# Dilated attention values: natural token tiles through a DRAM scratch, and the second scores of a group moved behind a projection half

## The chip, the cores and the metric

The kernel runs on one core of a Trainium2 chip. The metric is the device time of one execution in microseconds. Five engines run beside each other and meet only at semaphores: TensorE (PE: matmuls, and PEld: the loads of their stationary operand), VectorE (DVE), ScalarE (ACT), GpSimd (POOL) and the sync engine (SP), which here only issues transfers.

## What is computed

Two transformer blocks on 1024 tokens of width 1024, all in float32. The change lies in the second block, in its dilated attention: 24 heads of 64 in three groups of 8, with dilations 1, 4 and 16. Cut to what matters:

```python
DIL_CONFIGS = ((128, 1), (512, 4), (2048, 16))        # window, dilation
q_dil, k_dil, v_dil = h @ w_in[...]                    # 1536 columns each, 512 a group
q, k = rope(q), rope(k)                                # v is not roped
for g, (window, dilation) in enumerate(DIL_CONFIGS):
    # each query sees keys at offsets m * dilation, |m| <= window / (2 * dilation) = 64
    s = q @ k.T * D ** -0.5 ; p = exp(s - max) ; o = p @ v / sum(p)
out = softmax-weighted sum of the three groups
```

## The kernel before

The weights come in panels of 512 columns, in chunks of 512 KB, two chunks in staging. GpSimd splits each into a high and a low part, and a product is made of three passes (high by high, high by low, low by high). The normed input stands transposed in `h2T_hi` and `h2T_lo` (128 channels by 8 by 1024 tokens).

The dilated phase is a fixed list of **units** (`D_UNITS`, L476): for each group g its keys, values and queries, 8 units each, but 9 for group 0's values, so 73 units. A unit is one PSUM bank of 128x512 made by 24 matmuls (8 channel tiles by 3 passes) in two halves of 12, one half a **slot**. All engines walk through the same slots. `d_proj` (L1172) makes the half. Keys and queries have the weights as the stationary operand and 512 tokens moving. Values have the tokens as the stationary operand (`h2T`) and the 512 weight columns moving, so the output has tokens in partitions; a tile takes the 128 tokens that attention needs together (`value_tiles`, L450): for group 0 tiles shifted by 64, nine of them, for group 1 every fourth token, for group 2 every eighth. Banks rotate by three (`d_bank`), so unit u waits until unit u-3 was read (`d_read`).

After a unit, ScalarE copies it out (L1746 to L1760). A value unit goes straight into its tile of `vd` (named `v_dil`). A key or query unit goes into `ts` (`rope_in`, one buffer); SP then issues four transfers of 64 KB that swap the halves of each head into `rot` (`rope_swapped`, one buffer; `swap_halves`, L599), and VectorE multiplies by the sine table and adds to the cosine product (`rope_cos` L2265, `rope_sin` L2276). The next copy into `ts` waits for the swap (`swapped`), and the next swap waits until `rot` was used (`roped`).

Attention is cut into 16 **steps** a group (two heads, two query tiles). Steps begin some slots behind their query unit (`STEP_LAG`, L498). `d_scores` (L1197) waits for the roped queries and for the masking of the step before (`d_masked`), because all steps score into the same two banks. VectorE masks and takes the maximum (`d_soft`, L2286), ScalarE exponentiates (`d_exp`, L1725), TensorE transposes one slot later (`d_transposes`) and multiplies by the values two slots later (`d_values`). In a slot TensorE does the step's scores, the projection half, the values of the step two slots ago and the transposes of the step one slot ago; for the first step of a group the scores stand behind the half instead (L1247).

SP's loop (L668) does for each slot: the swaps of the unit before, the stores of the step two slots before, and in the first four units of each panel one weight chunk. Its queue is strictly in order.

Of the kernel before, what the change touches and what calls it, by code (L numbers as in the profile page):

```python
# [29 lines left out]
P = 128  # L30
# [67 lines left out]
def hybrid_blocks_kernel(nc, x, w_in, pool_w, pool_scale, attn_sinks, w_out, norm_pre, norm_post,  # L98
# [24 lines left out]
        "probs_copied": (("swa_pT", 16), ("d_pT", 48)),  # L123
        "values_summed": (("swa_valued", 16), ("d_valued", 48)),
        "values_copied": (("swa_out", 16), ("d_out", 48)),
        "pool_in_out": (("pool_c", 80), ("pool_spill", 64)),
    }
    for t in range(TT):
        shared[f"rows_in{t}"] = ((f"x_in{t}", 16),)
    for b in range(2):  # L130
        shared[f"x_tile_in{b}"] = ((f"x_back{b}", 64), (f"x1_back{b}", 64))
        shared[f"tile_out{b}"] = ((f"x1_out{b}", 64), (f"d_store{b}", 768))
# [76 lines left out]
    v_d = nc.dram_tensor("v_mla_scr", [S, 2 * H1 * HD], F32, kind="Internal").ap()  # L209
    am_d = nc.dram_tensor("amla_scr", [512, S], F32, kind="Internal").ap()  # L210
    dd_d = nc.dram_tensor("dilout_scr", [512, S], F32, kind="Internal").ap()
    dil_d = [nc.dram_tensor(f"dil{g}_scr", [S, 512], F32, kind="Internal").ap() for g in range(3)]
    st_d = [nc.dram_tensor(f"dil_stat{g}_scr", [S, STAT], F32, kind="Internal").ap() for g in range(2)]

# [225 lines left out]
    def tile_start(g, t):  # L440

        return ((P * t, 1), (t // 2 + 4 * P * (t % 2), 4), (t, 8))[g]

    def spread(start, step):
        return lambda h, k: h[:, k, start:start + step * (P - 1) + 1:step]

    def group_toks(g, t):
        return spread(*tile_start(g, t))

    def value_tiles(g):  # L450

        if g:
            return [(t, group_toks(g, t)) for t in range(TT)]
        starts = [0] + [P * t - HD for t in range(1, TT)] + [S - P]
        return [(t, spread(s_, 1)) for t, s_ in enumerate(starts)]

    def window(g, t):

# [6 lines left out]
        if t in (0, TT - 1):  # L465
# [7 lines left out]
    DIL_AT = 40  # L473
    OM_AT = 1

    D_UNITS = [(g, kind, t) for g in range(3) for kind in "kvq"  # L476
               for t in range(len(value_tiles(g)) if kind == "v" else 2 * 4)]
    N_D = len(D_UNITS)

    def rope_units(u):  # L480

        return sum(kind != "v" for _, kind, _ in D_UNITS[:u])

    def d_step(g, i):
        return 4 * 4 * g + i
# [28 lines left out]

    def d_bank(u):

        return (u + 2) % 3

    def gate_bank(u):

# [44 lines left out]
    def _(sp):  # L565
# [33 lines left out]
        def swap_halves(u):  # L599

            r = rope_units(u)
            sp.wait_ge(*after("d_copied", r + 1))
            if r:
                sp.wait_ge(*after("roped", r))
            for b in range(4):
                sp.dma_start(rot[32 * b:32 * b + 32, :], ts[32 * (b ^ 1):32 * (b ^ 1) + 32, :]).then_inc(sem("swapped"), 16)

        def d_rows(g, t):
            start, step = tile_start(g, t)
            return dil_d[g][start:start + step * (P - 1) + 1:step, :]  # L610
# [57 lines left out]
        for slot in range(D_SLOTS):  # L668
            u = slot // 2
            if slot % 2 == 0 and u in panel_start:  # L670
                place, start = slot, panel_start[u]
            done = unit_before(slot)
            if done and done[3] != "v":
                swap_halves(done[0])
            if slot - 2 in step_at:
                g, i = step_at[slot - 2]
                d_store(g, i)
                if i == 15 and g < 2:
                    stats_store(g)
            if (slot - place) % 2 and (slot - place) // 2 < 4 and u < N_D:  # L680
                load_chunk(start + (slot - place) // 2)
# [116 lines left out]
    def _(pe):  # L798
# [373 lines left out]
        def d_proj(slot):  # L1172

            u, part = divmod(slot, 2)
            g, kind, t = D_UNITS[u]
            name = f"{kind}{g}"
            s = index[name] % 2
            bank = ps[:, d_bank(u), :]
            if part == 0:
                if t == 0:  # L1180
                    panel_ready(name)
                if u >= 3:
                    pe.wait_ge(*after("d_read", u - 2))
            j, n = divmod(t, 2)
            for k in range(KT // 2 * part, KT // 2 * (part + 1)):
                if kind == "v":
                    toks = value_tiles(g)[t][1]
                    pairs = [(toks(a, k), b[:, s, k, :]) for a, b in ((h2h, wh), (h2h, wl), (h2l, wh))]
                else:
                    pairs = [(b[:, s, k, P * j:P * j + P], a[:, k, COLS * n:COLS * n + COLS])  # L1190
                             for a, b in ((h2h, wh), (h2l, wh), (h2h, wl))]
                for i, (a, b) in enumerate(pairs):
                    m = pe.matmul(bank, a, b, start=(k == 0 and i == 0), stop=(k == KT - 1 and i == 2))  # L1193
            if part == 1:
                m.then_inc(sem("d_done"), 1)
# [31 lines left out]
        def d_values(g, i):  # L1227
            n = d_step(g, i)
            j, tiles = step_of(g, i)
            if i == 0:  # L1230
                pe.wait_ge(*after("d_read", D_UNITS.index((g, "q", 0))))
            pe.wait_ge(*after("d_pT", n + 1))
            if n >= 1:
                pe.wait_ge(*after("d_out", n))
            c = 0
            for b, t in enumerate(tiles):
                blocks = window(g, t)[3]
                for a in range(2):
                    h, o = 2 * j + a, HD * (2 * b + a)
                    for kb, (_, _, vt, r0, nr) in enumerate(blocks):  # L1240
                        m = pe.matmul(ps[:, 7, o:o + HD], pTd[r0:r0 + nr, c, :],  # L1241
                                      vd[r0:r0 + nr, vt, HD * h:HD * h + HD], start=(kb == 0), stop=(kb == len(blocks) - 1))
                        c += 1
            m.then_inc(sem("d_valued"), 1)

        for slot in range(D_SLOTS):
            first = slot in step_at and step_at[slot][1] == 0  # L1247
            if slot in step_at and not first:
                d_scores(*step_at[slot])
            if slot < 2 * N_D:  # L1250
# [142 lines left out]
    def _(act):  # L1393
# [352 lines left out]
        for slot in range(D_SLOTS):  # L1746
            done = unit_before(slot)
            if done:
                u, r, g, kind, t = done
                if kind == "v" and t == 0:  # L1750
                    act.wait_ge(*after("d_read", u))
                    if g:
                        act.wait_ge(*after("d_valued", d_step(g, 0)))
                act.wait_ge(*after("d_done", u + 1))
                if kind == "v":
                    act.activation(vd[:, t, :], ps[:, d_bank(u), :], ACT.Copy).then_inc(sem("d_read"), 1)
                else:
                    if r:
                        act.wait_ge(*after("swapped", 64 * r))
                    act.activation(ts[:], ps[:, d_bank(u), :], ACT.Copy,  # L1760
                                   scale=HD ** -0.5 if kind == "q" else 1.0).then_inc(sem("d_copied"), 1)
            if slot in step_at:
                d_exp(*step_at[slot])
            if slot == D_SLOTS - 2:
# [700 lines left out]
```

## Time and profile before

| | |
|---|---|
| Median of 3 runs | 1717.63 us (1717.46 to 1717.9) |
| Profiled execution | 1716.55 us, span 1714.8 us |
| TensorE busy | 1685.3 us, 98% of the span |
| VectorE, ScalarE, GpSimd busy | 794.8, 586.3, 507.9 us |
| Dilated phase on TensorE | about 558 to 1140 us of the span |
| Bytes moved | 178.20 MB, mean 104 GB/s |

A busy time of TensorE adds up overlapping records less their overlap, so a record's length isn't the distance to the next matmul. A time in the views counts from the start of the span. "Idle before" is how long the engine stood before an instruction, with the one that released it. PEclk 1.00 means that the granted clock is the full 2.4 GHz, which it is in nearly all of this trace.

### The profile page before, as it was taken

Reading aid. Unit: us, or ns where it says so; the run is one execution under the profiler, and the core shown is the slowest. Engines: PE = TensorE matmul, PEld = TensorE weight load, DVE = VectorE, ACT = ScalarE, POOL = GpSimd, SP = SyncE. Lnnn points to the kernel's source line nnn. Section 1 sums busy time; section 2 is a strip of 40 time slices with the busy share of each in tenths; the row PEclk is TensorE's granted clock in tenths of the full one; section 3 lists DMA queues with packets and bytes.
Section 4 is the critical chain, followed back from the end, with each engine's and each line's share of the span. In section 5 each row is a group of like instructions: output and inputs, shape, how many; then the busy total and the mean of one; then the engine's idle time right before and its main releaser. Section 6 shows DMA issues by size and latency. Waiting matters only on the chain.

```text
span 1714.8 us, 22451 instructions
## 1 busy us (share of the span) xinstructions
PE 1685.3 (98%) x8753; PEld 1412.5 (82%) x8753; DVE 794.8 (46%) x1214; ACT 586.3 (34%) x1337; POOL 507.9 (30%) x400
## 2 busy tenths in 40 slices
PE   7999999999999999999999999999999999999998
PEld 6778778889878787888978889788787999988886
DVE  4330366344352213554166541645521888855714
ACT  5101456334333102441135310442113777741211
POOL 6125033023333333021220223015313744534310
PEclk9999999999999999999999999999999999999999
DMA  5113022233267422113131232227465525226332
GB/s 204 50 64 108 13 62 70 87 118 93 74 217 268 117 62 59 50 50 85 56 84 38 72 82 60 69 54 266 139 227 162 143 61 139 53 68 212 108 114 98
DMA packets 99290, 178.20 MB, mean 104 GB/s; under 512 B 16200, under 2 KB 36080, under 8 KB 99056
## 3 DMA queue, kind: packets, MB, share of 16 engines
q1 hardware_dynamic: 63280, 95.31, 20.0%
q10 hardware_dynamic: 35904, 81.44, 13.6%
q8 instruction: 70, 1.15, 0.3%
q14 instruction: 36, 0.29, 0.1%
HBM read 115.49 MB, written 48.63 MB: 96 GB/s over the span
## 4 chain that ended last, share of the span: by engine, by line
PE 95%; DVE 2%; ACT 1%; DMA 1%; issue 0%; SPq 0%; POOL 0%; ACTq 0%; POOLq 0%; DVEq 0%
PE ps L1193 23%; PE ps L1107 15%; PE ps L813 14%; PE ps L1045 5%; PE ps L1360 5%; PE ps L1300 5%; PE ps L1241 4%; PE ps L947 4%; PE ps L1330 3%; PE ps L1313 3%; PE ps L868 3%; PE ps L1209 2%; PE ps L1222 2%; PE ps L999 2%; PE ps L972 1%; PE ps L846 1%
## 5 line engine op out<-in xcount | busy, mean ns | idle before, releaser
L700 POOL TENSOR_SCALAR w_hi<-w_stage 128x1024 fp32r<-128x1024 f32 (+3 forms) x140 | 126.6, 911 | 997.7 <-PE ps L1193 361.1
L707 POOL TENSOR_TENSOR w_lo<-w_stage,w_hi 128x1024 fp32r<-128x1024 f32 (+3 forms) x140 | 270.1, 1937 | 8.9
L1193 PE MATMUL ps<-h2T_hi,w_hi 128*128 128x512 f32 x384 | 156.5, 408 | 0.7 <-ACT gate_tiles L1608 0.7
L1107 PE MATMUL ps<-h2T_hi,w_hi 128*128 128x512 f32 x384 | 154.2, 402 | 0.3 <-issue 0.3
L1193 PE MATMUL ps<-h2T_hi,w_lo 128*128 128x512 f32 x384 | 152.0, 396 | 0.0
L1107 PE MATMUL ps<-h2T_hi,w_lo 128*128 128x512 f32 x384 | 151.6, 395 | 0.0
L1193 PE MATMUL ps<-h2T_lo,w_hi 128*128 128x512 f32 x384 | 151.2, 394 | 0.0
L1107 PE MATMUL ps<-h2T_lo,w_hi 128*128 128x512 f32 x384 | 151.1, 393 | 0.0
L1735 ACT ACTIVATE probs_dil<-probs_dil,dil_stats_out 128x256 f32<-128x256 f32 (+2 forms) x192 | 87.6, 457 | 135.4 <-DVE dil_stats_out L2301 135.4
L1300 PE MATMUL ps<-k_mla,q_mla 128*128 128x512 f32 x384 | 104.0, 406 | 0.0
L2393 DVE TENSOR_REDUCE small<-ps 128x1 f32<-128x1024 f32 x64 | 77.7, 1214 | 54.8 <-PE ps L1300 54.8
L2273 DVE SCALAR_TENSOR_TENSOR qT_dil<-ps,cos_table_T 128x512 f32<-128x512 f32 x24 | 23.2, 967 | 166.9 <-ACT rope_in L1760 166.9
L732 POOL TENSOR_SCALAR p_mla<-p_mla,small 128x1024 f32<-128x1024 f32 x64 | 71.7, 1120 | 88.1 <-DVE small L2386 87.9
L1193 PEld LDWEIGHTS ps<-h2T_hi,w_hi 128*128 128x128 f32 x384 | 72.0, 188 | 26.6 <-issue 9.2
L2380 DVE TENSOR_TENSOR pT_mla_lo<-ps,pT_mla_hi 128x512 fp32r<-128x512 f32 x128 | 81.9, 680 | 14.0 <-ACT pT_mla_hi L1848 14.0
L1848 ACT ACTIVATE pT_mla_hi<-ps 128x512 fp32r<-128x512 f32 x128 | 69.7, 596 | 52.2 <-PE ps L1313 52.0
L1107 PEld LDWEIGHTS ps<-h2T_hi,w_lo 128*128 128x128 f32 x384 | 72.1, 188 | 18.1
L1193 PEld LDWEIGHTS ps<-h2T_hi,w_lo 128*128 128x128 f32 x384 | 72.2, 188 | 17.6
L1107 PEld LDWEIGHTS ps<-h2T_hi,w_hi 128*128 128x128 f32 x384 | 72.1, 188 | 17.1 <-issue 0.4
L1241 PEld LDWEIGHTS ps<-v_dil,probsT_dil 128*128 128x128 f32 (+1 forms) x640 | 80.8, 191 | 6.4 <-ACT probsT_dil L1744 0.5
L1107 PEld LDWEIGHTS ps<-h2T_lo,w_hi 128*128 128x128 f32 x384 | 72.1, 188 | 16.4
L2280 DVE TENSOR_TENSOR rope_swapped<-rope_swapped,sin_table_T 128x512 f32<-128x512 f32 x48 | 43.8, 912 | 89.6 <-DMA rope_swapped<-rope_in 89.6
(296 smaller groups left out, 3814.1 us busy)
## 6 DMA issues: line engine op xcount, KB each, us to landing
w_stage<-in_w_in SPq DMA_DIRECT2D x76, 512.0 KB, 3.9
rope_swapped<-rope_in SPq DMA_DIRECT2D x192, 64.0 KB, 2.0
w_stage<-in_w_out SPq DMA_DIRECT2D x16, 512.0 KB, 3.8
gate_scr<-gate_tiles ACTq DMA_DIRECT2D x16, 512.0 KB, 3.5
gates<-gate_scr ACTq DMA_DIRECT2D x32, 256.0 KB, 3.6
dil_scr<-dil_out SPq DMA_DIRECT2D x96, 64.0 KB, 1.6
dil_nums<-dil_scr ACTq DMA_DIRECT2D x24, 256.0 KB, 4.0
x_back<-in_x ACTq DMA_DIRECT2D x8, 512.0 KB, 3.6
```

The costliest lines, as they stand in the source:

```text
L700: last = nc.gpsimd.tensor_scalar(hi_, raw_, 1.0, 0.0, ALU.mult, ALU.add)
L707: last = nc.gpsimd.tensor_tensor(lo_, raw_, hi_.bitcast(F32), ALU.subtract)
L813: m = pe.matmul(acc, a, b, start=(i == 0 and j == 0), stop=(i == len(pairs) - 1 and j == 2))
L1045: m = pe.matmul(ps[:, Y_BANKS[t % 4] + half, :], a[:, k, tk], b[:, s, k, :], start=(k == 0 and j == 0), stop=(k == KT - 1 and j == 2))
L1107: m = pe.matmul(ps[:, gate_bank(u), :], a[:, s, k, P * m_:P * m_ + P], b[:, k, COLS * n:COLS * n + COLS], start=(k == 0 and j == 0), stop= ...
L1193: m = pe.matmul(bank, a, b, start=(k == 0 and i == 0), stop=(k == KT - 1 and i == 2))
L1241: m = pe.matmul(ps[:, 7, o:o + HD], pTd[r0:r0 + nr, c, :], vd[r0:r0 + nr, vt, HD * h:HD * h + HD], start=(kb == 0), stop=(kb == len(blocks ...
L1300: m = pe.matmul(ps[:, 2 * (i % 2) + n, :], Q[:, a, q], K[:, b, COLS * n:COLS * n + COLS], start=(j == 0), stop=(j == 2))
L1360: m = pe.matmul(ps[:, u % 8, :], a, b, start=(k == 0 and j == 0), stop=(k == 3 and j == 2))
L1735: act.activation(p_, p_, ACT.Exp, bias=o[:, h:h + 1], accum_out=o[:, H1 + h:H1 + h + 1]).then_inc(sem("d_exp"), 1)
L2380: nc.vector.tensor_tensor(PTl[dst], ps[:, 4 + half, :].rearrange("p (j c) -> p j c", c=P), PTh[dst].bitcast(F32), ALU.subtract).then_inc(s ...
L2393: nc.vector.tensor_reduce(rstd[:, j % 8:j % 8 + 1], ps[:, 2 * (j % 2):2 * (j % 2) + 2, :].rearrange("p b c -> p (b c)"), AX_X, ALU.max, ne ...
```

## The change

Value tiles of all groups become the eight natural tiles of 128 consecutive tokens, so group 0 has one unit less and the phase 72 units; the stationary operand is no longer shifted or strided. ScalarE copies a value unit into `ts` (now shared with the queries and keys), after the store or swap of the unit before. SP stores the 256 KB to a DRAM scratch `vd_d` (`store_values`), and loads tiles of `vd` from there with the shift or stride in the row address (`load_values`, 25 loads in all; `tiles_loaded` says after which unit which tiles come). At the last value unit of group 0 these are 3 tiles, of group 1 five, of group 2 four, and four more follow the first query unit of group 2. These stand in SP's queue behind the store of that unit and ahead of the swaps of the next. `d_values` waits for the loads. The second step's scores of each group stand behind the projection half as the first's do.

```diff
+    vd_d = nc.dram_tensor("v_dil_scr", [S, 512], F32, kind="Internal").ap()
-    def value_tiles(g):
+    def value_rows(g):
         if g:
-            return [(t, group_toks(g, t)) for t in range(TT)]
-        starts = [0] + [P * t - HD for t in range(1, TT)] + [S - P]
-        return [(t, spread(s_, 1)) for t, s_ in enumerate(starts)]
+            return [tile_start(g, t) for t in range(TT)]
+        return [(0, 1)] + [(P * t - HD, 1) for t in range(1, TT)] + [(S - P, 1)]
-    D_UNITS = [(g, kind, t) for g in range(3) for kind in "kvq"
-               for t in range(len(value_tiles(g)) if kind == "v" else 2 * 4)]
+    D_UNITS = [(g, kind, t) for g in range(3) for kind in "kvq" for t in range(TT)]
+    def tiles_loaded(g, kind, t):
+        if kind == "v" and g == 0:
+            return [t - 1] if 0 < t < TT - 1 else [TT - 2, TT - 1, TT] if t else []
+        if kind == "v" and g == 1:
+            return [2 * (t - 4)] if 4 <= t < TT - 1 else [6, 1, 3, 5, 7] if t == TT - 1 else []
+        if g == 2 and (kind, t) in (("v", TT - 1), ("q", 0)):
+            return list(range(4, TT)) if kind == "q" else list(range(4))
+        return []
+        def store_values(u):
+            g, _, t = D_UNITS[u]
+            sp.wait_ge(*after("d_read", u + 1))
+            if g and t == 0:
+                sp.wait_ge(*after("v_moved", 16 * (9, 17)[g - 1]))
+            sp.dma_start(vd_d[P * t:P * t + P, :], ts[:]).then_inc(sem("v_stored"), 16)
+        def load_values(u):
+            g, kind, t = D_UNITS[u]
+            for tile in tiles_loaded(g, kind, t):
+                sp.wait_ge(*after("v_stored", 16 * (8 * g + (t if kind == "v" and t < TT - 1 else TT))))
+                if g:
+                    sp.wait_ge(*after("d_valued", d_step(g, 0)))
+                start, step = value_rows(g)[tile]
+                sp.dma_start(vd[:, tile, :], vd_d[start:start + step * (P - 1) + 1:step, :]).then_inc(sem("v_moved"), 16)
-            if done and done[3] != "v":
-                swap_halves(done[0])
+            if done:
+                (store_values if done[3] == "v" else swap_halves)(done[0])
+                load_values(done[0])
@@ d_proj
-                    toks = value_tiles(g)[t][1]
-                    pairs = [(toks(a, k), b[:, s, k, :]) for a, b in ((h2h, wh), (h2h, wl), (h2l, wh))]
+                    pairs = [(a[:, k, P * t:P * t + P], b[:, s, k, :]) for a, b in ((h2h, wh), (h2h, wl), (h2l, wh))]
@@ d_values
             if i == 0:
-                pe.wait_ge(*after("d_read", D_UNITS.index((g, "q", 0))))
+                pe.wait_ge(*after("v_moved", 16 * (9 + 8 * g)))
@@ TensorE's slots
-            first = slot in step_at and step_at[slot][1] == 0
+            first = slot in step_at and step_at[slot][1] < 2
@@ ScalarE's slots
-                if kind == "v":
-                    act.activation(vd[:, t, :], ps[:, d_bank(u), :], ACT.Copy).then_inc(sem("d_read"), 1)
-                else:
-                    if r:
-                        act.wait_ge(*after("swapped", 64 * r))
-                    act.activation(ts[:], ps[:, d_bank(u), :], ACT.Copy,
-                                   scale=HD ** -0.5 if kind == "q" else 1.0).then_inc(sem("d_copied"), 1)
+                if u and D_UNITS[u - 1][1] == "v":
+                    act.wait_ge(*after("v_stored", 16 * values_stored(u)))
+                elif u:
+                    act.wait_ge(*after("swapped", 64 * r))
+                act.activation(ts[:], ps[:, d_bank(u), :], ACT.Copy,
+                               scale=HD ** -0.5 if kind == "q" else 1.0).then_inc(sem("d_read" if kind == "v" else "d_copied"), 1)
```

## Rows read from the trace of the kernel before

**Rows 1.** The page: busy us, share of the span, instructions.

```profile
PE 1685.3 (98%) x8753; PEld 1412.5 (82%) x8753; DVE 794.8 (46%) x1214; ACT 586.3 (34%) x1337; POOL 507.9 (30%) x400
```

**Rows 2.** Weight loads of value units, groups 0 to 2: ns min/median/max, starts.

```profile
L1193 PEld LDWEIGHTS ps<-w_hi,h2T_hi x72: 187/188/192, 603.3 to 653.1; 128*128 128x128 f32 x72
...
L1193 PEld LDWEIGHTS ps<-w_lo,h2T_hi x64: 308/309/309, 810.4 to 854.9; 128*128 128x128 f32 x64
...
L1193 PEld LDWEIGHTS ps<-w_lo,h2T_hi x64: 324/329/336, 1008.7 to 1054.8; 128*128 128x128 f32 x64
```

**Rows 3.** Timeline of ScalarE, value copies: start, us, operation, idle before.

```profile
614.92 0.60 ACT L1756 ACTIVATE v_dil<-ps 128x512 f32<-128x512 f32 x1 [4.96 <-PE ps L1193]
...
654.28 0.60 ACT L1756 ACTIVATE v_dil<-ps 128x512 f32<-128x512 f32 x1 [5.02 <-PE ps L1193]
...
827.52 0.60 ACT L1756 ACTIVATE v_dil<-ps 128x512 f32<-128x512 f32 x1 [5.06 <-PE ps L1193]
...
855.78 0.60 ACT L1756 ACTIVATE v_dil<-ps 128x512 f32<-128x512 f32 x1 [5.05 <-PE ps L1193]
...
1026.39 0.60 ACT L1756 ACTIVATE v_dil<-ps 128x512 f32<-128x512 f32 x1 [5.24 <-PE ps L1193]
...
1055.78 0.60 ACT L1756 ACTIVATE v_dil<-ps 128x512 f32<-128x512 f32 x1 [5.29 <-PE ps L1193]
```

**Rows 4.** Timeline of TensorE: first, second, third scores of groups 0, 1, 2.

```profile
668.17 1.03 PE L1209 MATMUL ps<-kT_dil,qT_dil 64*128 64x192 f32 x8
...
670.46 1.13 PE L1209 MATMUL ps<-kT_dil,qT_dil 64*128 64x256 f32 x8 [1.26 <-DVE probs_dil L2294]
...
869.68 1.13 PE L1209 MATMUL ps<-kT_dil,qT_dil 64*128 64x256 f32 x8
872.21 1.13 PE L1209 MATMUL ps<-kT_dil,qT_dil 64*128 64x256 f32 x8 [1.39 <-DVE probs_dil L2294]
...
877.13 1.14 PE L1209 MATMUL ps<-kT_dil,qT_dil 64*128 64x256 f32 x8
...
1075.28 0.71 PE L1209 MATMUL ps<-kT_dil,qT_dil 64*128 64x128 f32 x8
...
1080.92 0.71 PE L1209 MATMUL ps<-kT_dil,qT_dil 64*128 64x128 f32 x8
```

**Rows 5.** Timelines of ScalarE (last exponential of step 0), then VectorE (rope).

```profile
673.40 0.19 ACT L1735 ACTIVATION_READ_ACCUMULATOR probs_dil<-probs_dil,dil_stats_out 128x1 f32 x1
...
867.24 1.09 DVE L2284 TENSOR_TENSOR qT_dil<-qT_dil,rope_swapped 128x512 f32<-128x512 f32 x1
...
1073.07 1.20 DVE L2284 TENSOR_TENSOR qT_dil<-qT_dil,rope_swapped 128x512 f32<-128x512 f32 x1
...
1078.19 0.69 DVE L2280 TENSOR_TENSOR rope_swapped<-rope_swapped,sin_table_T 128x512 f32<-128x512 f32 x1 [0.62 <-DMA rope_swapped<-rope_in]
```

**Rows 6.** Transfers by line: queue, count, KB each, median us from issue to landing.

```profile
rope_swapped<-rope_in SPq DMA_DIRECT2D x192, 64.0 KB, 2.0
...
dil_nums<-dil_scr ACTq DMA_DIRECT2D x24, 256.0 KB, 4.0
...
q_mla<-q_rope_scr SPq DMA_DIRECT2D x48, 64.0 KB, 3.9
...
zm_scr<-gate_tiles ACTq DMA_DIRECT2D x4, 512.0 KB, 2.7
```

**Rows 7.** Timeline of SP: swaps of group 1's first two query units.

```profile
862.01 2.41 SPq L606 DMA_DIRECT2D rope_swapped<-rope_in  x4
...
868.40 3.04 SPq L606 DMA_DIRECT2D rope_swapped<-rope_in  x4
```

**Rows 8.** Windows: us, busy of the five engines, PEclk, DMA share, GB/s.

```profile
860.00:862.00 2.00, 2.00 (x10) 1.61 (x9) 0.00 (x0) 0.60 (x1) 1.92 (x2) 1.00 0.73 190
...
1156.00:1158.00 2.00, 2.00 (x14) 1.68 (x12) 0.00 (x0) 0.55 (x3) 0.00 (x0) 1.00 0.94 330
```

More of the change, by code:

```diff
@@ L125, in hybrid_blocks_kernel @@
         "values_copied": (("swa_out", 16), ("d_out", 48)),
-        "pool_in_out": (("pool_c", 80), ("pool_spill", 64)),
+        "pool_in_out": (("pool_c", 80), ("pool_spill", 64), ("v_moved", 400)),
     }
@@ L129, in hybrid_blocks_kernel @@
         shared[f"rows_in{t}"] = ((f"x_in{t}", 16),)
+    shared["rows_in7"] += (("v_stored", 16 * 3 * TT),)
     for b in range(2):
@@ L442, in tile_start @@
         return ((P * t, 1), (t // 2 + 4 * P * (t % 2), 4), (t, 8))[g]
[L444 to L448, printed above, removed]
-    def value_tiles(g):
+    def value_rows(g):
         if g:
-            return [(t, group_toks(g, t)) for t in range(TT)]
-        starts = [0] + [P * t - HD for t in range(1, TT)] + [S - P]
-        return [(t, spread(s_, 1)) for t, s_ in enumerate(starts)]
+            return [tile_start(g, t) for t in range(TT)]
+        return [(0, 1)] + [(P * t - HD, 1) for t in range(1, TT)] + [(S - P, 1)]
     def window(g, t):
@@ L482, in rope_units, with values_stored @@
         return sum(kind != "v" for _, kind, _ in D_UNITS[:u])
+    def values_stored(u):
+        return sum(kind == "v" for _, kind, _ in D_UNITS[:u])
+    def tiles_loaded(g, kind, t):
[6 more added lines that the diff above has]
+        return []
     def d_step(g, i):
@@ L515, in d_bank @@
     def d_bank(u):
-        return (u + 2) % 3
+        return (u - N_D) % 3
     def gate_bank(u):
@@ L1751, in _ @@
                     act.wait_ge(*after("d_read", u))
-                    if g:
-                        act.wait_ge(*after("d_valued", d_step(g, 0)))
                 act.wait_ge(*after("d_done", u + 1))
-                if kind == "v":
-                    act.activation(vd[:, t, :], ps[:, d_bank(u), :], ACT.Copy).then_inc(sem("d_read"), 1)
-                else:
-                    if r:
-                        act.wait_ge(*after("swapped", 64 * r))
-                    act.activation(ts[:], ps[:, d_bank(u), :], ACT.Copy,
-                                   scale=HD ** -0.5 if kind == "q" else 1.0).then_inc(sem("d_copied"), 1)
+                if u and D_UNITS[u - 1][1] == "v":
[4 more added lines that the diff above has]
+                               scale=HD ** -0.5 if kind == "q" else 1.0).then_inc(sem("d_read" if kind == "v" else "d_copied"), 1)
             if slot in step_at:
```

## The prediction

> **What bounds the kernel now.** I read the busy times first: TensorE (PE) is busy for 1685.3 of 1714.8 us [rows 1]. So a change pays only by what it takes from TensorE's queue or from a gap in it. Transfers, ScalarE, VectorE and the sync queue count only where they make TensorE wait. The record of one 128x512 matmul lasts about 0.4 us, but matmuls overlap, so I don't price by that mean. I price a projection unit (24 matmuls) by the distance between two ScalarE copies in the value stretches, where each copy waits for TensorE alone [rows 3].
>
> **The removed ninth tile.** Group 0's values fall from nine units to eight. From the copy at 614.92 to the one at 654.28 are 7 units: 39.36 / 7 = 5.62 us each [rows 3]. TensorE runs through without a gap there, so the whole unit counts: **-5.62 us**.
>
> **Plain instead of strided weights.** In groups 1 and 2 the stationary operand of a value unit is every fourth or eighth token of `h2T`. Its load takes 309 ns at a step of 4 and 329 ns at a step of 8, against 188 ns plain [rows 2]. Most of that hides behind the moving 512 columns, as the copies show: group 1 has (855.78 - 827.52) / 5 = 5.65 us a unit, group 2 (1055.78 - 1026.39) / 5 = 5.88 us [rows 3]. With plain tiles both should come to group 0's 5.62: 8 x 0.03 = 0.24 us and 8 x 0.26 = 2.08 us, together **-2.3 us**. Bounds: 0 if the slower pace isn't from the stride, -2.5 us if the units come down to 5.60.
>
> The Trainium skill, SBUF — State Buffer, section on the DMA port swizzle, says that reads are at full speed while a 16-byte line is hit more than once and that fp32 can be strided by up to 4 for free. The load at step 4 disagrees (309 ns), though the unit it belongs to is nearly free. By that rule group 1 would give nothing and group 2 all, which is 0.24 us from my sum.
>
> **The detour through DRAM, value stretches.** Copies stay as long as they are (0.60 us, PSUM to SBUF), but go to the single buffer `ts`, so the copy of a unit now waits until the previous tile has been stored. The trace has no 256 KB store from SBUF; the nearest are 512 KB at 2.7 us and 64 KB swaps at 2.0 us [rows 6]. I take 2.2, near the swaps, with ends 2.0 and 2.7. The cycle copy 0.6, store 2.2 and two hand-overs of 0.1 (my estimate) is 3.0 us against 5.62 a unit: hidden, cost **0**, bounds 0 and 0, since the upper end also gives 3.5. The sync queue now waits for each unit in this stretch; behind it stand weight chunks, of which only four belong to eight units of 5.62 us, and a panel is first used one stretch later. The 24 stores and 25 loads of 256 KB are 12.8 MB of extra traffic beside 178 MB. Group 0's loads follow tile by tile and hide likewise.
>
> **The detour, at the turn to the queries.** Call C the end of the last value copy: 855.78 + 0.60 = 856.38 in group 1 [rows 3]. The sync queue now issues that tile's store at C+0.1, waits until it has landed (C+2.3), issues 5 loads in group 1 (3 in group 0, 4 in group 2), then one weight chunk of 512 KB, then the four swaps of the first query unit. A swap issue takes 2.41 / 4 = 0.6 us [rows 7]; at that pace 5 loads end at C+5.3 and the chunk at C+5.9, while the swaps issue at C+5.6 today. So the queue itself costs 0.3 us. The data matter more: strided 2 KB rows moved at 330 GB/s with engines 94% busy, so 351 GB/s full, and weight chunks with swaps at 190 / 0.73 = 260 GB/s [rows 8]. If the loads start to flow 1.5 us after issue, five take to C+3.8+3.7 = C+7.5 and the chunk to C+9.5; at 260 GB/s for the loads too it is C+8.8 and C+10.8. The swaps, which land at C+9.4 today (last issue 863.8 plus 2.0), would land by C+10.2 to C+11.5: late by 0.8 to 2.1 us. A 64 KB load in a crowd of others took 3.9 us instead of 2.0 [rows 6], which supports such a delay.
>
> What that costs: roped queries were ready at 867.24 + 1.09 = 868.33 [rows 5], the first scores began at 869.68 [rows 4], a cushion of 1.35 us. So the first scores start 0 to 0.75 us late. But the next swap waits for these roped queries (issued at 868.40 [rows 7]), VectorE's second masking waits for that swap, and TensorE's third scores wait for the masking. I estimate it as finished 7.65 us after the roped queries (4.5 to the landing of swaps that issue for 3.0 us [rows 7], 1.8 for sine and sum, 1.3 for the mask), so at 876.8 to 878.1 against 877.13 today [rows 4]. Group 1: bounds -0.6 (no delay at all, below) and +1.0; I take **-0.1**.
>
> Group 2 scores only after two query units. Its second unit is roped at 1073.07 + 1.20 = 1074.27 [rows 5], the scores begin at 1075.28 [rows 4], a cushion of 1.0 us. First unit: 4 loads, no delay in the queue, landing late by 0 to 1. After its swaps come 4 more loads and a chunk, 1.5 MB in all, then the second swap at C+12. At 351 GB/s they are gone before that swap's data come, at 260 GB/s they end near C+16.5 and delay it by about 1 us. The scores there already hang on this chain (sine at 1078.19 waits for a swap [rows 5]), so a delay costs in full: bounds 0 and +2.0, I take **+0.3**. In group 0, with 3 loads, the queue is free at C+4.7 and the data by C+8.5: **0**. The first value product waits for its tiles at no cost. It comes at least two slots (5.6 us) behind the first scores: in group 1 those stand at 869.68 = C+13.3, so from C+18.9 on, in group 2 (C = 1056.38) at 1075.28 = C+18.9, so from C+24.5 on [rows 3, 4]. The last load is issued by C+5.3 and C+10.4; 256 KB loads of such strided rows land in 4.0 us [rows 6], and even in a crowd by C+9 and C+17.
>
> **Second scores behind a projection half.** Today the second scores of a group wait for the masking of the first: TensorE stands idle 1.26 us in group 0 and 1.39 in group 1 [rows 4]. The half of 12 matmuls (2.8 us) now lies between, and the idle time is gone. But the transposes of the first step then come 1.1 + 2.8 + 1.1 = 5.0 us after the first scores began, and their exponentials are finished at 673.40 + 0.19 = 673.59, 5.4 us after 668.17 [rows 4, 5]: about 0.5 us comes back as a wait. Group 0 keeps **-0.75**. In group 1 it would keep -0.6, which stands in its line above. In group 2 the third scores (1080.92) hang on VectorE, which adds the third unit's sine before the second masking: 1078.19 + 0.69 + 1.2 + 0.75 = 1080.8 [rows 4, 5]. Whatever TensorE gains, it waits there: **0**.
>
> **Sum.** -5.62 - 2.3 - 0.75 - 0.1 + 0.3 = **-8.5 us**. The profiled execution took 1716.55 us (span 1714.8 and 1.75 around it), so it would take 1708.1; the median of the runs is 1717.63, 1.1 above it, which gives **1709.1 us**, and that is my prediction.
>
> **Rivals.**
> 1. *The swaps queue behind the loads.* If the sync queue's transfers are handled strictly in order and the new loads run slowly, group 1 and group 2 lose up to 2 us each more than I take and group 0 its 0.75: -8.5 + 5 = -3.5, so about 1714; the middle of the case is 1712. For it: 3.9 against 2.0 us [rows 6]. Against: the four query copies are a unit apart and 1.35 us of cushion stand ahead of the first scores. Chance 0.22. The Trainium skill, DMA: Bandwidth & Descriptors, section on queues, rings and completion order, says that one issuing engine has one ring on each of 16 DMA engines and that descriptors are taken in ring order. No row here shows that order directly; by it this rival gets the upper delays above, 1712.
> 2. *The transfers pass freely.* No swap is late: -5.62 - 2.3 - 0.75 - 0.6 - 0 = -9.3, with 5.60 a unit -9.6: 1708. Chance 0.20, and it lies inside my range.
> 3. *The stride isn't the cause of the slow units* (or plain value tiles are slower for another reason): -8.5 + 2.3 = -6.2: 1711.4. Against it is the jump of the load from 188 to 329 ns just there [rows 2]. Chance 0.05.
> 4. *Slower than before: the single buffer paces the value units.* If store and hand-overs take over 5.0 us, the cycle is longer than a unit; beyond 4.8 us of landing each unit pays the excess 24 times. At 5.6 us it is 24 x 0.8 = 19 us, so -8.5 + 19 = +10.5: 1728. It decides from 4.8 us, against 2.0 to 2.7 in the rows [rows 6]. The Trainium skill, same page, section on the anatomy of one DMA, gives 2.0 us plus bytes at 436 GB/s for another issue path; as an estimate 2.6 us for 256 KB, which leaves it hidden too. Chance 0.04.
>
> **Numbers.** Forecast (-7.5 to -9.2) 0.49, rival 1 0.22, rival 2 0.20, rival 3 0.05, rival 4 0.04. 0.2% (3.4 us) is about what a measurement of this kernel can tell from no change. Faster beyond that: forecast, rivals 2 and 3 and most of rival 1: 0.90; within: the poor end of rival 1: 0.05; slower: rival 4 and a rest for a wait that I haven't seen: 0.05. Range: 1706.5 (rival 2 and 1 us more) to 1714 (the end of rival 1).
>
> **What the profile after would show.** Value units 5.62 us apart in all three groups and all plain loads at 188 ns confirm the first two terms. The landing time of the value stores (I say 2.2 us) decides rival 4. The start of the first scores after the last value copy is 13.3 us in group 1 today; more means rival 1. A wait of some 0.5 us ahead of the first transposes in groups 0 and 1 shows the traded wait. I am wrong if TensorE shows waits inside the value stretches, or if the gap between the last value copy and the third scores grows by over 1 us in group 1 or 2.

## The result and the profile after

The changed kernel takes **1720.46 us** (median of 15 runs, 1716.67 to 1724.16) against 1717.15 us (15 runs, 1715.45 to 1719.23): ratio 1.0023, 95% interval 1.0016 to 1.0030. It is slower by 3.3 us; I had forecast 8.5 us less. The profiled execution took 1719.46 us with a span of 1717.6.

The two gains that I had priced are there. First TensorE's busy time as in [rows 1], then the weight loads of value units in groups 1 and 2 as in [rows 2], then value copies of groups 0 to 2 as in [rows 3] (last one of a group each, with ScalarE's idle time before it).

```profile
PE 1681.3 (98%) x8729; PEld 1389.7 (81%) x8729; DVE 798.6 (46%) x1214; ACT 585.9 (34%) x1336; POOL 509.8 (30%) x400
```

```profile
L1219 PEld LDWEIGHTS ps<-w_lo,h2T_hi x64: 187/188/192, 807.3 to 851.6; 128*128 128x128 f32 x64
...
L1219 PEld LDWEIGHTS ps<-w_lo,h2T_hi x64: 187/188/192, 1008.7 to 1052.9; 128*128 128x128 f32 x64
```

```profile
650.38 0.60 ACT L1783 ACTIVATE rope_in<-ps 128x512 f32<-128x512 f32 x1 [5.03 <-PE ps L1219]
...
852.51 0.60 ACT L1783 ACTIVATE rope_in<-ps 128x512 f32<-128x512 f32 x1 [5.03 <-PE ps L1219]
858.11 0.60 ACT L1783 ACTIVATE rope_in<-ps 128x512 f32<-128x512 f32 x1 [5.00 <-PE ps L1219]
865.66 0.60 ACT L1783 ACTIVATE rope_in<-ps 128x512 f32<-128x512 f32 x1 [6.95 <-DMA rope_swapped<-rope_in]
...
1053.84 0.60 ACT L1783 ACTIVATE rope_in<-ps 128x512 f32<-128x512 f32 x1 [5.03 <-PE ps L1219]
```

All loads are at 188 ns. The last value copies stand at 650.38, 852.51 and 1053.84 against 654.28, 855.78 and 1055.78 [rows 3]: earlier by 3.90, 3.27 and 1.94 us, although this execution started the dilated phase 1.73 us late (first copy at 566.21 instead of 564.48; more on this below). Counted from the phase's start that is 5.63, 5.00 and 3.67 us. So the kernel gains in the key and value stretches and loses in the query stretches. From a group's last value copy to the next group's first copy it takes 105.76 us instead of 104.86 in group 0 and 105.97 instead of 102.68 in group 1, and from group 2's last value copy to the last scores 95.08 instead of 89.56: 0.90, 3.29 and 5.52 us more. The third copy shown (858.11) is the first query unit's, and the next one (865.66) waits for a transfer, which none of these did in group 1 before.

Now the waits at the first scores, as in [rows 4]: TensorE's first scores of groups 0, 1 and 2, with the idle time before each and what ended it; then a matmul right behind the last.

```profile
665.24 1.03 PE L1235 MATMUL ps<-kT_dil,qT_dil 64*128 64x192 f32 x8 [0.90 <-DVE qT_dil L2307]
...
869.51 1.14 PE L1235 MATMUL ps<-kT_dil,qT_dil 64*128 64x256 f32 x8 [3.04 <-DVE qT_dil L2307]
...
1075.56 0.71 PE L1235 MATMUL ps<-kT_dil,qT_dil 64*128 64x128 f32 x8 [2.15 <-DVE qT_dil L2307]
...
1077.02 0.63 PE L1219 MATMUL ps<-h2T_hi,w_lo 128*128 128x512 f32 x1
```

Three waits for roped queries that didn't exist before. What delays them in group 1 is seen in three timelines: the sync queue (store of the last value tile, five loads, a weight chunk, the four swaps), VectorE (sine, then sum, of the first query unit) and GpSimd (the split of that chunk).

```profile
853.13 0.32 SPq L622 DMA_DIRECT2D v_dil_scr<-rope_in  x1
855.14 2.22 SPq L632 DMA_DIRECT2D v_dil<-v_dil_scr  x5
857.41 0.42 SPq L675 DMA_DIRECT2D w_stage<-in_w_in  x1
858.73 2.44 SPq L614 DMA_DIRECT2D rope_swapped<-rope_in  x4
```

```profile
865.60 0.74 DVE L2303 TENSOR_TENSOR rope_swapped<-rope_swapped,sin_table_T 128x512 f32<-128x512 f32 x1 [5.69 <-DMA rope_swapped<-rope_in]
866.38 3.08 DVE L2307 TENSOR_TENSOR qT_dil<-qT_dil,rope_swapped 128x512 f32<-128x512 f32 x1
```

```profile
864.75 1.05 POOL L727 TENSOR_SCALAR w_hi<-w_stage 128x1024 fp32r<-128x1024 f32 x1 [5.15 <-DMA w_stage<-in_w_in]
865.89 2.65 POOL L734 TENSOR_TENSOR w_lo<-w_stage,w_hi 128x1024 fp32r<-128x1024 f32 x1
```

With C = 852.51 + 0.60 = 853.11 as the end of the last value copy, the swaps are issued from C+5.6 on, as before, but have landed only at C+12.5 (865.60), not at C+9.5. Then the sum takes 3.08 us instead of 1.09 [rows 5]: it ends only after GpSimd's subtraction (865.89 to 868.54) is over. In the kernel before (C = 856.38), VectorE's sine, which starts when the swap has landed, stands at C+9.5; the split of that chunk began at C+6.7 instead of C+11.6 and its subtraction was over (866.66) when the sum began (867.24 [rows 5]):

```profile
865.89 1.31 DVE L2280 TENSOR_TENSOR rope_swapped<-rope_swapped,sin_table_T 128x512 f32<-128x512 f32 x1 [2.69 <-DMA rope_swapped<-rope_in]
...
863.12 1.04 POOL L700 TENSOR_SCALAR w_hi<-w_stage 128x1024 fp32r<-128x1024 f32 x1 [0.23 <-DMA w_stage<-in_w_in]
864.25 2.41 POOL L707 TENSOR_TENSOR w_lo<-w_stage,w_hi 128x1024 fp32r<-128x1024 f32 x1
```

The swap's 3.0 us and the sum's 2.0, less the cushion of 1.35 and 0.6 that the sine was shorter, give the wait of 3.04.

Group 2 loses more, and there the delay runs over two units. VectorE's sum of the first query unit, then the swaps of the second (C = 1053.84 + 0.60 = 1054.44; 1056.38 before):

```profile
1066.39 3.27 DVE L2307 TENSOR_TENSOR qT_dil<-qT_dil,rope_swapped 128x512 f32<-128x512 f32 x1
```

```profile
1069.73 2.41 SPq L614 DMA_DIRECT2D rope_swapped<-rope_in  x4
```

The first unit's swap has landed at C+11.2 instead of C+9.5, and its sum takes 3.27 us instead of 1.19, again beside GpSimd's subtraction (1065.89 to 1068.62). The second unit's swaps may only be issued after that sum, so they come at C+15.3 instead of C+12.1. They land 3.9 us after that, as before, although four loads and a chunk stand ahead of them. So the 3.2 us come from the first unit's chain; less the cushion of 1.0 they are the wait of 2.15.

Windows of the transfers in group 1, and of TensorE's clock in group 2 (columns as in [rows 8]):

```profile
857.00:859.00 2.00, 2.00 (x10) 1.63 (x9) 0.16 (x1) 0.60 (x1) 1.92 (x2) 1.00 0.99 326
859.00:861.00 2.00, 2.00 (x11) 1.59 (x10) 0.91 (x1) 0.00 (x0) 0.61 (x1) 1.00 0.93 313
861.00:863.00 2.00, 2.00 (x10) 1.64 (x9) 0.00 (x0) 0.00 (x0) 0.00 (x0) 1.00 1.05 308
863.00:865.00 2.00, 2.00 (x10) 1.59 (x9) 0.00 (x0) 0.00 (x0) 0.24 (x1) 1.00 0.87 248
...
1076.00:1078.00 2.00, 2.00 (x11) 1.49 (x8) 1.90 (x5) 0.03 (x1) 0.00 (x0) 0.62 0.29 66
1078.00:1080.00 2.00, 2.00 (x7) 1.57 (x6) 0.51 (x1) 1.62 (x8) 0.00 (x0) 0.53 0.62 113
```

From 857 to 865 the transfer engines are full at 248 to 326 GB/s. Over the whole time from the first load's issue to the landing of the swap (855.14 to 865.60) the mean is 249 GB/s, which is 2.6 MB: the five loads, the chunk, the swaps and nearly all of the next weight chunk too, which SP issued at 861.21 (C+8.1, as before) right behind the swaps. Behind the idle stretch of 3.04 us in group 1 the granted clock stays at 1.00. Behind that of 2.15 us in group 2 it is 0.62 and 0.53 in the two windows, that is 3.4 us at its lower level of 1.2 GHz: a 512-column matmul then comes every 0.43 us instead of every 0.233 and its record lasts 0.63 us. The mean granted clock of all 15 runs is 0.996 to 0.998, that of the kernel before 0.998 to 1.000.

Last, the new transfers as in [rows 6]: stores land in 2.0 us, loads in 3.3 us.

```profile
v_dil<-v_dil_scr SPq DMA_DIRECT2D x25, 256.0 KB, 3.3
v_dil_scr<-rope_in SPq DMA_DIRECT2D x24, 256.0 KB, 2.0
```

### The profile page after: what moved, and what is told of

It reads as the page before. It is cut to its first block, busy times and chain, and to the rows that moved or that the text cites. A ratio compares the mean times of both kernels' runs of the same rounds, so it can differ in the third digit from the quotient of the medians.

```text
span 1717.6 us, 22490 instructions
## 1 busy us (share of the span) xinstructions
PE 1681.3 (98%) x8729; PEld 1389.7 (81%) x8729; DVE 798.6 (46%) x1214; ACT 585.9 (34%) x1336; POOL 509.8 (30%) x400
## 4 chain that ended last, share of the span: by engine, by line
PE 91%; DVE 3%; ACT 2%; DMA 2%; SPq 1%; issue 1%; POOL 0%; ACTq 0%; DVEq 0%; POOLq 0%
PE ps L1219 20%; PE ps L1134 15%; PE ps L840 14%; PE ps L1072 5%; PE ps L1386 5%; PE ps L1326 5%; PE ps L974 4%; PE ps L1267 4%; PE ps L1356 4%; PE ps L1339 3%; PE ps L895 3%; PE ps L1235 2%; PE ps L1248 2%; PE ps L1026 2%; DMA rope_swapped<-rope_in 1%; SPq L614 1%
## 5 line engine op out<-in xcount | busy, mean ns | idle before, releaser
L1783 ACT ACTIVATE rope_in<-ps 128x512 f32<-128x512 f32 x72 | 42.9, 595 | 259.3 <-DMA rope_swapped<-rope_in 120.8
L2303 DVE TENSOR_TENSOR rope_swapped<-rope_swapped,sin_table_T 128x512 f32<-128x512 f32 x48 | 38.5, 802 | 102.0 <-DMA rope_swapped<-rope_in 101.9
```

## The experiments

Theory A says that a swap in flight together with value loads lands late, and that TensorE pays for it with idle time. Theory B blames the detour through DRAM as such, theory C the order of the second scores. Two additions are tested apart: VectorE's collision with GpSimd, and the clock behind an idle stretch. Each ratio is to the kernel before, run on the same chip. The edits are cut to the lines that matter.

**Second scores alone** (scores_only), on the kernel before.

```diff
-            first = slot in step_at and step_at[slot][1] == 0
+            first = slot in step_at and step_at[slot][1] < 2
```

> The kernel before with the second scores of each group behind the projection half as the only edit. Theory A: TensorE's waits of 1.26, 1.39 and 0.86 us for the masking go, about half comes back ahead of the first transposes; 0.5 to 1.5 us less than before, 1716. Theory C (this edit is what made the kernel slower): 1719 to 1721.

Measured 1716.88 us, ratio 0.9999 (0.9991 to 1.0008). The waits of 1.26 and 1.39 us at the second scores are gone; two waits of 1.1 us together come back ahead of the first transposes. Theory C falls, and this edit is worth nothing that can be measured.

**Second scores undone** (scores_undone), on the changed kernel (the same line, the other way).

> The changed kernel with the second scores of each group ahead of the projection half again. Theory A: the late swaps stay, so it is as slow as the changed kernel or up to 1.5 us slower: 1720 to 1722. Theory C: it drops to 1709, since the removed unit and the plain weights then count in full.

Measured 1722.47 us, ratio 1.0033 (1.0020 to 1.0045). It doesn't drop to 1709, as theory C wanted. Its eight runs have mean clocks of 0.992 to 0.996, and the profiled one (1717.57 us) is the fastest of them. In its profile the idle stretch at the first scores (2.67 us in group 1) is followed at once by that at the second (1.38 us).

**Loads behind the first query unit's swaps** (swaps_first).

```diff
+        if kind == "q" and t == 0:
+            return ([TT - 1, TT], [1, 3, 5, 7], [0, 1, 2, 3])[g]
+        if g == 2 and kind == "q" and t == 1:
+            return [4, 5, 6, 7]
```

> The changed kernel, but at each turn to the queries the loads of value tiles that wait for the last store stand behind the first query unit's swaps (group 0: 2, group 1: 4, group 2: 4 and another 4 behind the second unit's swaps). Theory A (the swaps queue behind the loads): the first swap lands about 9.5 us after the last value copy as before, TensorE's waits for roped queries (0.90, 3.04 and 2.15 us) vanish, and the kernel takes 8 to 9 us less than the one before: 1708.5. Theory B (the loss comes from the detour as such: the store, the single buffer, 12.8 MB more): no change against the changed kernel, 1720. Theory C (the second scores cost it): 1720 too.

Measured 1720.65 us, ratio 1.0021 (1.0012 to 1.0030): none of the gain that I gave theory A. The timelines of VectorE and then TensorE in group 1 say why.

```profile
862.84 1.14 DVE L2305 TENSOR_TENSOR rope_swapped<-rope_swapped,sin_table_T 128x512 f32<-128x512 f32 x1 [2.85 <-DMA rope_swapped<-rope_in]
...
872.21 0.69 DVE L2305 TENSOR_TENSOR rope_swapped<-rope_swapped,sin_table_T 128x512 f32<-128x512 f32 x1 [1.93 <-DMA rope_swapped<-rope_in]
872.93 3.09 DVE L2309 TENSOR_TENSOR qT_dil<-qT_dil,rope_swapped 128x512 f32<-128x512 f32 x1
```

```profile
866.49 1.13 PE L1237 MATMUL ps<-kT_dil,qT_dil 64*128 64x256 f32 x8
870.55 1.13 PE L1237 MATMUL ps<-kT_dil,qT_dil 64*128 64x256 f32 x8
877.37 2.08 PE L1237 MATMUL ps<-kT_dil,qT_dil 64*128 64x256 f32 x8 [3.83 <-DVE probs_dil L2319]
```

The first scores start without a wait. But the second unit's swaps, issued from 865.18 to 867.6, now stand behind four loads and have landed only at 872.21, the sum takes 3.09 us beside GpSimd again, VectorE's second masking stands behind that sum, and TensorE waits 3.83 us at the third scores. The delay went one unit on. My expectation forgot that the second unit's swap is just as urgent. It also gives a number for the collision: 872.93 to 876.02 against GpSimd's subtraction, which ended at 875.09.

**GpSimd held back** (pool_hold).

```diff
+                    if ci == 2 and p in (index["k1"], index["k2"], index["gm0"]):
+                        g = (index["k1"], index["k2"], index["gm0"]).index(p)
+                        pool.wait_ge(*after("roped", 16 * g + 9))
```

> The changed kernel, but GpSimd holds the split of the third weight chunk at each turn to the queries until the first query unit is roped, so that VectorE's sum of that unit meets no work of GpSimd. If half of the delay is VectorE waiting for GpSimd (the sum took 2.77, 3.08 and 3.27 us instead of 0.69 to 1.2): the sums take 0.7 to 1.2 us again, the first scores start 2 us sooner in each group, TensorE's waits fall from 0.90, 3.04, 2.15 to about 0, 1.0, 0.2, and the kernel gains 4 to 6 us: 1715. The swaps still land as late as in the changed kernel. If the long sum is not from GpSimd: no change, 1720.

Measured 1721.93 us, ratio 1.0028 (1.0017 to 1.0039). VectorE's sums of the first and of the second unit in group 1, then TensorE's first and third scores there:

```profile
867.69 1.07 DVE L2310 TENSOR_TENSOR qT_dil<-qT_dil,rope_swapped 128x512 f32<-128x512 f32 x1
...
873.96 3.10 DVE L2310 TENSOR_TENSOR qT_dil<-qT_dil,rope_swapped 128x512 f32<-128x512 f32 x1
```

```profile
868.81 1.13 PE L1238 MATMUL ps<-kT_dil,qT_dil 64*128 64x256 f32 x8 [1.27 <-DVE qT_dil L2310]
...
878.41 1.13 PE L1238 MATMUL ps<-kT_dil,qT_dil 64*128 64x256 f32 x8 [2.56 <-DVE probs_dil L2320]
```

The collision is shown: without GpSimd's work the first sum takes 1.07 us and the wait falls from 3.04 to 1.27. But GpSimd's work is only moved: the split behind the held one (its subtraction from 873.47 to 876.14) now meets the second unit's sum, so the time isn't saved. The expected gain was wrong for the same reason as above. The Trainium skill, SBUF — State Buffer, section on who interferes with whom, says that a VectorE instruction with two SBUF inputs and a GpSimd instruction that reads SBUF exclude each other in full; the trace agrees (3.10 against 1.07 us).

**Loads issued by ScalarE** (act_queue), on its own queue, at the same moment (C+2.0 in both).

```diff
+                    for tile in tiles_loaded(g_, k_, t_):
+                        start, step = value_rows(g_)[tile]
+                        act.dma_start(vd[:, tile, :], vd_d[start:start + step * (P - 1) + 1:step, :]).then_inc(sem("v_moved"), 16)
```

> The changed kernel, but the loads that wait for a group's last store are issued by ScalarE at the same moment as before by the sync queue (after that store has landed; group 2's second four ahead of the second query unit's copy). If order within one queue is the cause: the first swap of group 1 lands 9.5 to 10.5 us after the last value copy instead of 12.5, TensorE's wait there falls from 3.04 us to under 1, and the kernel gains 5 to 8 us: 1713. If the transfer engines as such are too busy whatever the queue: the swap lands at 12 to 12.5 again and the time stays at 1719 to 1721.

Measured 1720.41 us, ratio 1.0021 (1.0011 to 1.0032). VectorE's first sine in group 1 (C = 852.73), GpSimd's split of the chunk that SP issued ahead of the swaps, and a window of the transfers:

```profile
865.74 1.54 DVE L2311 TENSOR_TENSOR rope_swapped<-rope_swapped,sin_table_T 128x512 f32<-128x512 f32 x1 [6.21 <-DMA rope_swapped<-rope_in]
```

```profile
863.20 1.05 POOL L727 TENSOR_SCALAR w_hi<-w_stage 128x1024 fp32r<-128x1024 f32 x1 [3.98 <-DMA w_stage<-in_w_in]
```

```profile
861.00:863.00 2.00, 2.00 (x10) 1.59 (x9) 0.00 (x0) 0.00 (x0) 0.00 (x0) 1.00 1.06 279
```

The swap lands at C+13.0 from a queue that holds no value loads. So it needn't stand behind the loads in its own queue to be late: the transfer engines are full, whichever queue issues. What this run doesn't separate is the weight chunk, which still stands ahead of the swaps in SP's queue and itself landed only at C+10.5 instead of C+6.7. Whether the swaps are late by sharing the engines alone, or also by standing behind that late chunk, stays open.

**A quarter of the bytes** (quarter_loads). This kernel leaves out three quarters of the values in these loads.

```diff
+                w = 128 if g and (kind == "q" or t == TT - 1) else 512
+                sp.dma_start(vd[:, tile, 0:w], vd_d[start:start + step * (P - 1) + 1:step, 0:w]).then_inc(sem("v_moved"), 16)
```

> The changed kernel, but in groups 1 and 2 each load at the turn to the queries (5, 4 and 4) moves 128 of its 512 columns; the other three quarters of those values are left out. Number, place, queue and waits of all transfers stay. If the bytes are what delays the swaps: group 1's first swap lands 9.5 to 10.3 us after the last value copy instead of 12.5, its wait falls from 3.04 to under 0.5 us, group 2's from 2.15 to under 0.5, and the time falls to 1711 to 1713. If the number of transfers or the issue time delays them: it stays at 1719 to 1721.

Measured 1713.06 us, ratio 0.9978 (0.9969 to 0.9986). VectorE in group 1 (C = 852.31):

```profile
862.01 2.63 DVE L2304 TENSOR_TENSOR rope_swapped<-rope_swapped,sin_table_T 128x512 f32<-128x512 f32 x1 [2.91 <-DMA rope_swapped<-rope_in]
```

Same number, place and waits of transfers, but the swap has landed by C+9.7: the bytes of the loads are the cause of its delay. Of the waits, 0.85 us stays in group 1 and 0.51 in group 2 (I had expected under 0.5 for both), in group 1 because the chunk still comes later than before and its split now meets the sine (2.63 us instead of 1.3).

**Late loads** (late_loads). The loads wait until no urgent swap comes soon.

```diff
+        if kind == "q" and t == 1:
+            return ([TT - 1, TT], [1, 3, 5, 7], [0, 1, 2])[g]
+        if g == 2 and kind == "q" and t == 2:
+            return [3, 4, 5, 6, 7]
```

> The changed kernel, but the loads that wait for a group's last store stand where no swap comes soon after: behind the second query unit's swaps (group 0: 2, group 1: 4, group 2: 3), group 2's other 5 behind the third unit's. The work is the same. Theory A (a swap that stands behind loads is late, and TensorE pays): no swap is late, the first scores start 13.3 us (group 1) and 18.9 us (group 2) after the last value copy as before, the clock stays up, and the kernel takes 7 to 9 us less than before: 1709. Theory B (the detour costs as such): 1719 to 1721 again.

Measured 1712.37 us, ratio 0.9971 (0.9959 to 0.9983): 5.0 us less than before, 8 us less than the changed kernel, with all of the detour in place. Theory B falls, though the 1709 that I had expected isn't reached. TensorE's first three scores of group 1, then the third of group 2:

```profile
863.93 1.13 PE L1237 MATMUL ps<-kT_dil,qT_dil 64*128 64x256 f32 x8
867.99 1.13 PE L1237 MATMUL ps<-kT_dil,qT_dil 64*128 64x256 f32 x8
870.90 1.13 PE L1237 MATMUL ps<-kT_dil,qT_dil 64*128 64x256 f32 x8
...
1074.39 0.71 PE L1237 MATMUL ps<-kT_dil,qT_dil 64*128 64x128 f32 x8 [1.89 <-DVE probs_dil L2319]
```

No wait at these scores in group 1, and none at those of group 0. Group 2 has a wait of 1.89 us, where three loads stand ahead of the third unit's swap.

**The same with the scores' order undone** (late_loads_undone).

> The same with the second scores of each group ahead of the projection half, as in the kernel before. Alone, the edit of the scores changed nothing (1716.88 against 1716.99), so theory A gives the time of late_loads plus 0 to 1 us: 1709 to 1710. If the order of the scores matters more once the swaps are on time: up to 1.5 us more than late_loads.

Measured 1713.61 us, ratio 0.9973 (0.9962 to 0.9984): 0.0002 in the ratio and 1.2 us in the median above late_loads, with intervals that overlap. The scores' edit is worth nothing here either that can be told, and 1709 to 1710 was again too low.

**Group 2's loads behind the chunks** (loads_after_chunk).

```diff
+            return ([TT - 1, TT], [1, 3, 5, 7], [])[g]
+        if g == 2 and kind == "q":
+            return ([0, 1], [], [2, 3, 4, 5, 6, 7])[t] if t < 3 else []
@@ SP's slots: behind the store of a value unit as before, and behind the chunk
+            if slot % 2 and unit_before(slot - 1) and unit_before(slot - 1)[3] == "q":
+                load_values(unit_before(slot - 1)[0])
```

> late_loads with group 2's loads placed otherwise: 2 behind the chunk that follows the first query unit's swaps, none between the second and third unit's swaps, 6 behind the chunk that follows the third's. In late_loads the third unit's sine came 2.85 us after its swaps were issued instead of 1.45, and TensorE waited 1.89 us at the third scores. If the three loads ahead of it are the cause, that wait falls to about 0.5 us and the kernel gains 1 to 2 us over late_loads: 1711. If not, 1712 again.

Measured **1711.49 us**, ratio 0.9970 (0.9959 to 0.9981), the lowest median of this study: 5.6 us less than before. Third scores and first value product of group 2:

```profile
1071.26 0.71 PE L1240 MATMUL ps<-kT_dil,qT_dil 64*128 64x128 f32 x8 [0.38 <-DVE probs_dil L2322]
1075.92 1.10 PE L1272 MATMUL ps<-v_dil,probsT_dil 128*128 128x64 f32 x8 [0.94 <-DMA v_dil<-v_dil_scr]
```

The wait of 1.89 us is down to 0.38; the last loads are now 0.94 us late for the product. The step over late_loads (0.9 us in the median) is within the intervals, so of the two kernels neither is shown to be the faster.

**Idle time alone** (stall_g1), on the kernel before.

```diff
+            if (g, i) == (1, 0):
+                pe.wait_ge(*after("swapped", 64 * (16 + 8 + 2)))
```

> The kernel before; TensorE's first scores of group 1 also wait for the second query unit's swap, which makes it stand idle for some 3.3 us and changes nothing else. If an idle stretch costs only its length: 2 to 3.3 us more than before, 1719 to 1720.3, granted clock 0.999. If it also lowers the granted clock behind it, as in the changed kernel's group 2 (half speed for some 4 us): 1.7 us more than that, 1721 to 1722, and the mean clock falls to 0.998.

Measured 1722.94 us, ratio 1.0035 (1.0023 to 1.0047), mean clocks 0.996 and 0.997. First and second scores of group 1, and windows of 4 us:

```profile
873.32 1.61 PE L1211 MATMUL ps<-kT_dil,qT_dil 64*128 64x256 f32 x8 [2.61 <-issue]
876.30 2.08 PE L1211 MATMUL ps<-kT_dil,qT_dil 64*128 64x256 f32 x8 [1.38 <-DVE probs_dil L2296]
```

```profile
868.00:872.00 4.00, 2.71 (x12) 1.86 (x10) 2.22 (x3) 0.55 (x1) 2.28 (x2) 1.00 0.44 136
872.00:876.00 4.00, 1.61 (x8) 0.91 (x8) 1.04 (x2) 0.00 (x0) 1.11 (x1) 0.73 0.56 154
876.00:880.00 4.00, 3.70 (x12) 2.58 (x13) 3.93 (x7) 2.08 (x8) 0.00 (x0) 0.50 0.00 0
880.00:884.00 4.00, 4.00 (x24) 3.20 (x24) 1.78 (x3) 2.15 (x9) 0.00 (x0) 0.92 0.00 0
```

The median is 5.6 us higher (1722.94 against 1717.37). The profiled execution also had a clock dip at 232 to 240 us, in the first block, where its code is unchanged, so I take the price from the dilated phase alone: it is 5.06 us longer than in the kernel before. The idle stretch itself is 2.61 us. The other 2.4 us come while the clock is at its lower level, by the windows for 6.8 us, part of which TensorE spends waiting at the second scores anyway.

## Why the prediction was wrong

**Right.** The removed unit was worth 5.63 us (I said 5.62). The strided units gave 0.26 us in group 1 (from the first key copy to the last value copy 96.38 instead of 96.64 us; I said 0.24) and 1.96 in group 2 (95.36 instead of 97.32; I said 2.08). Stores landed in 2.0 us (I said 2.2). Early in a value stretch some copies did wait for one (three in group 1, from 823.24 to 830.88), but TensorE never did, so rival 4 fell.

**The step that failed** is "the detour, at the turn to the queries". I took 0, -0.1 and +0.3 us for groups 0, 1 and 2; rival 1 added up to 2 us each in groups 1 and 2, and ended at 1714. Measured in the query stretches were +0.90, +3.29 and +5.52 us. The phase as a whole, from its first copy to its last scores, took 582.71 us instead of 580.86: +1.85 where -8.5 was forecast. Three things were left out or mis-sized there.

1. *The bytes in flight.* I had the swap late by 0.8 to 2.1 us; it was 3.0. The 1.8 MB of loads and chunk that I costed were right, and the full engines moved 248 to 326 GB/s, about my two rates. But the swaps' own 0.25 MB and the next weight chunk shared the engines with them: 2.6 MB had passed before the swap landed. The Trainium skill, DMA: Bandwidth & Descriptors, section on queues, rings and completion order, says that descriptors are taken in ring order, and I had put that behind rival 1. It isn't what holds the swaps behind the loads here: with the loads on another queue the swap came as late. It may still hold them behind the chunk in their own queue; no run separates that.
2. *VectorE beside GpSimd.* My chain from landed swap to roped query had fixed durations from one row (1.8 us). But that row was short because GpSimd happened to be done. The loads also delayed the weight chunk, so its split began 4.9 us later and moved onto the sum: 3.08 instead of 1.09 us. I counted SP's queue and the transfer engines behind the new loads, and not who works when the delayed chunk lands. In group 2 I had looked for the delay in the four loads ahead of the second unit's swaps; these cost nothing there. But the first unit, whose swap I had landing 0 to 1 us late, was roped 3.2 us late, and the second unit's swaps wait for it.
3. *The clock.* I priced a wait at its length. Idle stretches of 2.15 us and more in the dilated phase were followed by half clock in nine of the eleven that the profiles of this case show (not behind the 3.04 of the changed kernel and a 2.56 in pool_hold). What it costs can be compared in group 1's query stretch (102.68 us in the kernel before): an idle stretch of 3.04 us without a fall of the clock made it 3.29 us longer, one of 3.05 with 3.4 us at half clock (act_queue) 4.45, and one of 2.61 with 6.8 us at half clock (stall_g1) 4.86. The length doesn't decide alone: a wait of 1.69 us at some 236 us in the first block, the same in all twelve profiles, was followed by 3.4 us at half clock in four of them. The changed kernel's profile has that dip and the one of the kernel before hasn't; it goes with the 1.73 us by which the phase began late, but doesn't explain them alone, since swaps_first began at 566.19 us without it. The starts range from 563.20 to 566.21 us over the twelve profiles, and no run ties this to the change.

A second, smaller step failed as well, the scores' order. I took -0.75 us in group 0 and had -0.6 in group 1's best case. With that edit alone the profile has 104.67 us instead of 104.86 in group 0's query stretch and 102.71 instead of 102.68 in group 1's: 0.2 us and nothing. The waits were traded as I wrote (1.26 and 1.39 us gone, 0.38 and 0.75 back), but what takes the rest isn't isolated. In the medians the edit is worth 0.1 us with an interval of some 1.5 us to either side.

So the mechanism was on my list as rival 1, as a term of at most 5 us. The query stretches lost 9.7 us together, where I had summed a gain of 0.55. The price that I gave the rival had no second and third part, and my range ended where they begin.

**Still open.** In loads_after_chunk the profiled execution took 1708.95 us, near the sum's 1708.1, but by luck: it began the phase 1.28 us earlier than the kernel before did, and the phase itself is 6.9 us shorter, not 8.5. The median is 1711.49. Clock dips alone don't explain the difference between its runs: the one with a mean clock of 1.000 took 1711.49 too. Nor is it isolated why the waits of group 2 behind the third scores add up to some 2 us in the changed kernel (one of 1.08 us) and not before.

## What to carry to other kernels

A transfer that nobody waits for soon is free only if nobody's urgent transfer is in flight with it: count the bytes between two urgent ones, whatever queue they are on, and place bulk loads where the next urgent transfer is far. When a transfer is delayed, follow what its landing starts (here GpSimd's split) and ask which other engine's work it will now meet. And price a long TensorE wait (here 2.15 us and more) at up to twice its length, until a profile shows the clock staying up.

## What the hardware showed that I had not expected

- Half clock behind one idle stretch: 2.61 us idle made the phase 5.06 us longer; matmuls of 512 columns every 0.43 us instead of 0.233, for 3.4 us in the changed kernel and within 6.8 us in stall_g1.
- 64 KB swaps from a queue without any value load (a weight chunk still ahead of them) landed as late (13.0 us after the last value copy) as from the queue with five of them (12.5).
- A stationary operand strided by 16 or 32 bytes loads in 309 or 329 ns instead of 188, yet a unit of 24 such matmuls is only 0.03 or 0.26 us slower; that held when the stride was taken away.
- VectorE's 128x512 sum of two SBUF operands: 1.07 us alone, 3.1 us beside GpSimd's subtraction of 128x1024.
